# Fills and PSUM copies moved at the norm boundaries of a two-part transformer kernel's second half

## What is computed

```python
def second_block(x, mem, ...):
    mem_n = rms_norm_2(mem, mem_norm_gain)
    for layer in range(DEPTH):
        g = norm_gains[layer]
        hn = rms_norm_2(x, g[0])
        if layer % 2 == 0:
            y = mlstm_mixer(hn, ...)
        else:
            y = stick_breaking_mixer(hn, ...)
        x = x + rms_norm_2(y, g[1])
        y = memory_cross_attention(rms_norm_2(x, g[2]), mem_n, xa_w_q[layer], xa_w_kv[layer], xa_w_o[layer])
        x = x + rms_norm_2(y, g[3])
        y = swiglu_ffn(rms_norm_2(x, g[4]), ffn_w_gate_up[layer], ffn_w_down[layer])
        x = x + rms_norm_2(y, g[5])
    return x

def rms_norm_2(x, gain):
    y = x * lax.rsqrt(jnp.mean(x * x, axis=-1, keepdims=True) + RMS_EPS)
    return y * gain
```

## Time and profile before

| | us |
|---|---|
| median of three runs | 1744.31 |
| their lowest and highest | 1741.27, 1747.47 |
| the profiled execution | 1744.86 |
| its span, first to last instruction | 1743.1 |
| PE busy in the span | 1678.6 |
| DVE, ACT, POOL busy | 1161.3, 949.2, 331.8 |

### The profile page before, as it was taken

One profiled execution on the slowest core, in us unless ns is written; L12 is line 12 of the kernel. 1 busy time (PEld: TensorE's weight loads), 2 busy tenths in 40 slices (PEclk: granted clock), 3 DMA queues, 4 the chain that ended last, 5 costly groups with the idle time before them and its releaser, 6 DMA issues.

```text
span 1743.1 us, 32581 instructions
## 1 busy us (share of the span) xinstructions
PE 1678.6 (96%) x13166; PEld 1605.1 (92%) x13166; DVE 1161.3 (67%) x1964; ACT 949.2 (54%) x1717; POOL 331.8 (19%) x304
## 2 busy tenths in 40 slices
PE   7999999999999989999999999999999998989997
PEld 6998889999997889999999889999989998889996
DVE  7889886555577745556675556666686656476665
ACT  6676765644455646544655545544465644354443
POOL 0100110243412112335111101002232210000025
PEclk9999999999999999999999999999999999989999
DMA  5433334555522245555445434565554352335653
GB/s 203 135 112 122 110 109 146 169 171 177 175 96 79 91 133 195 183 189 185 146 135 167 145 110 157 170 184 188 163 167 143 113 161 97 119 117 168 190 181 108
DMA packets 76325, 257.47 MB, mean 148 GB/s; under 512 B 8464, under 2 KB 12560, under 8 KB 75920
## 3 DMA queue, kind: packets, MB, share of 16 engines
q1 hardware_dynamic: 76176, 255.39, 45.3%
HBM read 254.31 MB, written 1.05 MB: 147 GB/s over the span
## 4 chain that ended last, share of the span: by engine, by line
PE 79%; DVE 11%; ACT 6%; issue 3%; POOL 1%; DMA 0%; POOLq 0%; DVEq 0%; SPq 0%; ACTq 0%
PE pb L140 79%; DVE WL L159 3%; DVE TMP L171 2%; ACT SCR L149 2%; DVE SCR L171 2%; ACT WH L149 1%; ACT L156 1%; PE pb L143 1%; DVE SCR L159 1%; DVE HNL L171 1%; ACT ASH L149 1%; ACT TMP L149 0%; ACT SCR L150 0%; ACT Rbuf L149 0%; DVE ASL L171 0%
## 5 line engine op out<-in xcount | busy, mean ns | idle before, releaser
L159 DVE TENSOR_TENSOR WL<-RAW,WH 128x1024 fp32r<-128x1024 f32 (+4 forms) x514 | 606.6, 1182 | 13.3 <-ACT WH L149 13.0
L140 PE MATMUL pb<-HNH,WH 128*128 128x256 f32 (+1 forms) x2056 | 595.2, 289 | 4.9 <-issue 2.4
L149 ACT ACTIVATE WH<-RAW 128x1024 fp32r<-128x1024 f32 (+4 forms) x514 | 507.5, 989 | 151.1 <-PE pb L140 148.1
L140 PE MATMUL pb<-HNH,WL 128*128 128x256 f32 (+1 forms) x2056 | 584.6, 284 | 0.0
L140 PE MATMUL pb<-HNL,WH 128*128 128x256 f32 (+1 forms) x2056 | 584.4, 284 | 0.0
L140 PE MATMUL pb<-ASH,WH 128*128 128x256 f32 (+1 forms) x1560 | 453.0, 290 | 10.3 <-DVE WL L159 7.7
L140 PE MATMUL pb<-ASH,WL 128*128 128x256 f32 (+1 forms) x1560 | 444.6, 285 | 0.0
L140 PE MATMUL pb<-ASL,WH 128*128 128x256 f32 (+1 forms) x1560 | 444.1, 285 | 0.0
L140 PEld LDWEIGHTS pb<-HNH,WH 128*128 128x128 f32 x2056 | 389.5, 189 | 12.9 <-issue 5.6
L140 PEld LDWEIGHTS pb<-HNH,WL 128*128 128x128 f32 x2056 | 389.9, 190 | 0.0
L140 PEld LDWEIGHTS pb<-HNL,WH 128*128 128x128 f32 x2056 | 388.1, 189 | 1.1
(11 more groups left out here) (155 smaller groups left out, 1735.9 us busy)
## 6 DMA issues: line engine op xcount, KB each, us to landing
RAW<-in_w_gu SPq DMA_DIRECT2D x88, 512.0 KB, 3.9
RAW<-in_w_up SPq DMA_DIRECT2D x64, 512.0 KB, 3.5
RAW<-in_w_down SPq DMA_DIRECT2D x64, 512.0 KB, 3.5
RAW<-in_w_ssd SPq DMA_DIRECT2D x48, 512.0 KB, 3.5
RAW<-in_w_xkv SPq DMA_DIRECT2D x32, 512.0 KB, 3.9
RAW<-in_w_mlin SPq DMA_DIRECT2D x24, 512.0 KB, 3.6
RAW<-in_w_fd SPq DMA_DIRECT2D x32, 384.0 KB, 3.0
RAW<-in_w_sbqkv SPq DMA_DIRECT2D x24, 512.0 KB, 4.1
```

The lines of the kernel that those rows point to most:

```text
L140: return self.eng.matmul(o, l, r, start=start, stop=stop, skip_group_check=skip) if self.eng else Nothing()
L149: return self.eng.activation(o, i, f, bias=bias, scale=scale)
L159: return self.eng.tensor_tensor(o, a, b, op) if self.eng else Nothing()
```

## The change

`FIRSTS` becomes 1, 1, 1, 0 for mlo, xo0, fd0, sbo (before 3, 2, 2, 1), so `pe_rest` stands behind one fill, at sbo behind none. On PE all later fills then come in one run, and behind them all feeds of the next norm. On ACT `act_fill` is taken apart: `act_fill_begin` makes the high splits, `act_fill_end` waits for PE and copies. The splits of the first later fill stand ahead of the norms; behind norms 1, 3, 5, 7 come the copy of a fill and then the splits of the next one. On DVE the low splits of the first later fill stand ahead of the Newton step, those of the others ahead of gains 2, 4, 6. Instructions, data and the order of `PLAN` are the same.

```diff
-        FIRSTS = {"mlo": 3, "xo0": 2, "fd0": 2, "sbo": 1, "xo1": 0, "fd1": 0}
-
-        def fills_at(post, m):
-
-            rest = FILL[post][FIRSTS[post]:]
-            return rest[m // 2:m // 2 + 1] if m % 2 == 0 else []
+        FIRSTS = {"mlo": 1, "xo0": 1, "fd0": 1, "sbo": 0, "xo1": 0, "fd1": 0}
...
-        def act_fill(q, kind, l, m):
+        def act_fill_begin(q, kind, l, m):
             if kind == "k":
-                i, b = act_block(q, f"xkv{l}", 0, m, T2)
+                act_block(q, f"xkv{l}", 0, m, T2)
+            else:
+                act_split(q, v_blocks(q, l, m)[1])
+
+        def act_fill_end(q, kind, l, m):
+            if kind == "k":
+                i = AT[f"xkv{l}", 0, m]
                 q.wait_ge(*use[i])
                 if l:
                     q.wait_ge(*xs_[0, 3])
-                q.activation(KM[:, m, :], b, ACT.Copy).then_inc(*eva(i))
+                q.activation(KM[:, m, :], bank_of(i)[:, 0:T2], ACT.Copy).then_inc(*eva(i))
                 return
...
@@ def pe_post_norm
             pe_rest(q, post, T2)
-            for m in range(8):
-                for f in fills_at(post, m):
-                    pe_fill(q, *f)
-                if m and nxt:
-                    pe_feed(q, nxt, m - 1, T2, rms[post])
-            if nxt:
-                pe_feed(q, nxt, 7, T2, rms[post])
+            for f in fill[FIRSTS[post]:]:
+                pe_fill(q, *f)
+            for m in range(8 if nxt else 0):
+                pe_feed(q, nxt, m, T2, rms[post])
@@ def act_post_norm
-            for m in range(8):
-                for f in fills_at(post, m):
-                    act_fill(q, *f)
-                if m and nxt:
-                    act_norm(q, nxt, m - 1, x_added(post, m - 1), use[AT[HNFREE[nxt]]])
-            if nxt:
-                act_norm(q, nxt, 7, x_added(post, 7), use[AT[HNFREE[nxt]]])
+            for f in fill[:1]:
+                act_fill_begin(q, *f)
+            for m in range(8 if nxt else 0):
+                act_norm(q, nxt, m, x_added(post, m), use[AT[HNFREE[nxt]]])
+                if m % 2:
+                    for f in fill[m // 2:m // 2 + 1]:
+                        act_fill_end(q, *f)
+                    for f in fill[m // 2 + 1:m // 2 + 2]:
+                        act_fill_begin(q, *f)
@@ def dve_post_norm
-            fill, nxt, gi = FILL[post], NEXT[post], GAIN[post]
-            for f in fill[:FIRSTS[post]]:
+            fill, nxt, gi = FILL[post][FIRSTS[post]:], NEXT[post], GAIN[post]
+            for f in FILL[post][:FIRSTS[post]] + fill[:1]:
                 dve_fill(q, *f)
...
-                for f in fills_at(post, m):
-                    dve_fill(q, *f)
+                if m and m % 2 == 0:
+                    for f in fill[m // 2:m // 2 + 1]:
+                        dve_fill(q, *f)
```

More of the change, by code:

```diff
@@ L1821, in act_fill @@
                     q.wait_ge(*xs_[0, 3])
-                q.activation(KM[:, m, :], b, ACT.Copy).then_inc(*eva(i))
+                q.activation(KM[:, m, :], bank_of(i)[:, 0:T2], ACT.Copy).then_inc(*eva(i))
                 return
-            ids = v_blocks(q, l, m)
-            act_split(q, ids[1])
-            q.wait_ge(*use[ids[1]])
+            i = AT[f"xkv{l}", 0, 8 + 2 * m]
+            q.wait_ge(*use[i + 1])
             if l:
@@ L1829, in act_fill @@
             for t in range(2):
-                q.activation(VM[:, t, 256 * m:256 * m + 256], bank_of(ids[t])[:, 0:256], ACT.Copy).then_inc(*eva(ids[t]))
+                q.activation(VM[:, t, 256 * m:256 * m + 256], bank_of(i + t)[:, 0:256], ACT.Copy).then_inc(*eva(i + t))
+        def act_fill(q, *f):
+            act_fill_begin(q, *f)
+            act_fill_end(q, *f)
         def dve_fill(q, kind, l, m):
@@ L1863, in act_post_norm @@
         def act_post_norm(q, post):
-            fill, nxt = FILL[post], NEXT[post]
-            for f in fill[:FIRSTS[post]]:
+            fill, nxt = FILL[post][FIRSTS[post]:], NEXT[post]
+            for f in FILL[post][:FIRSTS[post]]:
                 act_fill(q, *f)
```

## The result

| | before | after |
|---|---|---|
| median of five runs, us | 1745.16 | 1736.58 |
| lowest and highest | 1741.27, 1747.47 | 1735.54, 1738.35 |
| the profiled execution | 1744.86 | 1738.35 |
| its span | 1743.1 | 1736.6 |

The ratio is 0.9954 with a 95% interval of 0.9939 to 0.9969: the changed kernel is faster by 8.6 us, between 5.4 and 10.6. The forecast was 1735.5 in a range of 1730 to 1741.

A forecast was written before the change was run, and what follows sets the result against it. PE, busy 96% of the span, was taken as the bound; gains 4.3 + 2.6 + 3.2 + 0.5 less 1.5 for one clock fall make 9.1 us, from 1744.31 to 1735.2, written as 1735.5, range 1730 to 1741.

The forecast's parts named there:

- xo0, 4.3: At xo0 sums start one block earlier, all five feeds find their squares, gate block ends 1087.1: gain 4.3 us.
- the price of five feeds, 1.66: At xo0 and mlo, five feeds ahead of the gate block counted as 1.66 us of PE work.
- fd0, 2.6: At fd0 the fills' end stays, the fifth feed waits, first block ends 1300.4 instead of 1303.05: gain 2.6 us.
- sbo, 3.2: At sbo sums precede the only fill, Newton starts 1442.65 instead of 1445.84, block ends 3.2 earlier: gain 3.2 us.
- one fall in the whole change: At mlo one fall of the granted clock behind a 2.77 us PE idle, charged at 1.5 us.
- mlo, 0.5 less 1.5 of clock: At mlo earlier sums bring a new 2.77 us PE wait: gain 0.5 us, less 1.5 for a clock fall.
- Rival 1: No clock fall is added at mlo: gain 10.6 us, time 1733.7; chance 0.26.
- rival 2: At xo0, fd0 and sbo DVE slips, and the clock falls a second time: gain 6.1, 1738.2 us; chance 0.20.
- Rival 3: At seven bank hand-overs copies behind the norms hold PE: 14.1 lost against 9.1, 1749.3 us; chance 0.04.
- Rival 4: At fd0 or sbo squares ahead of the first fill are late, Ln not earlier: gain 3.3, 1741.0; chance 0.08.
- three signs of being wrong: PE waits for copies at xo0 or fd0; sbo's first feed over 3 us after the fill; mlo's wait at every fill.

The follow-up runs named there:

- the kernel with filler: The changed kernel with six products of constants, results unused, ahead of mlo's second V fill, where PE waited for the copy; 1735.44 us, ratio 0.9955.

## Why the prediction was right, and where not

The time, 1736.58 against 1735.5, and the sum of 9.1 against 8.6 of the medians, came out within what can be measured. The terms, against the stretches:

- **xo0, 4.3; measured 3.94.** The chain was right: no wait of PE for a bank, a square or HNL, and no fall of the clock. About 1.5 of the gain is the block that ran at half clock before; in the nine kernels with earlier sums the clock did not fall here. The term that was mis-sized is the price of five feeds, 1.66. They take 1.97 (in the full rows 1084.06 to the first gate matmul at 1086.03). I had halved the 0.67 of two products, but two do not cost twice one. A product is two records, and all ten of the five feeds start 0.215 apart; only the last is followed by the gate matmul after 0.03. So n products ahead of a block take 0.215 (2n - 1) + 0.03: 0.67 for two, 1.11 for three (1091.36 to 1092.46 before), 1.97 for five. The same 0.3 is missing at mlo (994.88 to 996.85).
- **fd0, 2.6; measured 2.17.** The fills' end stood still, as said: the first feed is 16.15 after the start of the stretch, 16.05 before. The fifth feed does wait for its square, which ends 1.92 after that point (1.97 in the forecast; its row starts 1294.29 and lasts 0.40), though the grouped row of PE shows no bracket. The block begins at 2.32 (1295.09), as forecast, but takes 3.43 instead of 3.0. That is the 0.4: I had priced a block whose eight chunks all lie ready, and DVE was still writing HNL until 1298.0.
- **sbo, 3.2; measured 2.05, and 3.20 where the clock stayed up** (19.77 - 16.57, the kernel with filler; its sbo is the same code). From the first feed to the tail sums both take 8.07, so the fall in the kernel before cost nothing there. Every link is in the trace: the second split waits 2.02 for ACT, then Newton, then the chain as it was. What failed is the sentence on the clock: I charged one fall in the whole change and wrote of sbo only that it "keeps a stretch of sparse products". Before, the clock fell there too, but under feeds that were waiting anyway; in after it fell under the block. PE alone, of before and then of after:

```profile
1450.00:1452.00 2.00, 2.00 (x6) 0.50 0.00 0
```

```profile
1446.00:1447.00 1.00, 1.00 (x3) 0.62 0.00 0
1447.00:1448.00 1.00, 1.00 (x7) 0.50 0.00 0
1448.00:1449.00 1.00, 1.00 (x7) 0.50 0.00 0
1449.00:1450.00 1.00, 1.00 (x8) 0.67 0.00 0
```

- **mlo, 0.5 less 1.5 of clock, a loss of 1.0; measured 1.30.** The wait was forecast at 2.77 in one piece and is 2.57; the clock's price was 1.5 and is 1.51; the feeds took 0.3 more. That is 1.1, and 0.2 remain from small differences that I did not follow up.

Together 1.1 of sbo's clock, 0.4 at xo0, 0.4 at fd0 and 0.3 at mlo are 2.2, and 9.1 - 2.2 = 6.9 is the sum of the stretches. The medians gave 1.7 more than the stretches do, so that they came within 0.5 of the forecast is in part luck. No experiment settles which part of that is the first half's scatter and which is the clock's at sbo and xo1, where other executions of the same code are up to 1.5 shorter.

**The rivals.** Rival 1 (no fall) and rival 2 (a second fall) were both the right kind: a second fall that costs came, 1.1 at sbo, not at mlo. Rival 3, the ring at every bank, bit once, as the forecast had it; the other hand-over at mlo is 0.52, and xo0 and fd0 have none. Rival 4 is refuted by fd0's 2.17 and by the first feed of sbo 1.0 after the fill. None of the three signs of being wrong came: PE has no wait for a copy at xo0 or fd0, the first feed at sbo is 1.0 behind the fill, and the long wait at mlo does not recur.

**What I did not see** is that one edit of the three carries the gain. I costed the change as a whole at each boundary. Costed by edit, it would have shown the sums ahead of the fills as the gain, the run as 1.5 more, and the late copies as the cause of mlo's loss.

## To carry to other kernels

When a change bundles several moves, price each of them at each place: here one line gave 9.5 us at the boundaries, and the copies that were moved out of the way of the norms gave back 3.6 at the one boundary with two-bank fills behind each other. A copy that frees a bank may be put behind other work only if none of that work waits, by whatever engines, for the user of the bank. A wait of PE costs more than its length when the clock falls behind it, so compare the step of the block behind the wait too.

## What the runs showed of the hardware

- **The clock falls at a different moment in executions of the same instructions.** sbo with after's code took 16.57 (no fall), 17.70, 17.72 and 18.41 us. In the last of these the clock was 0.50 in 1444 to 1448, under the last feed and most of the block:

```profile
1444.00:1448.00 4.00, 3.53 (x15) 0.50 0.00 0
```

xo1, the same code in every kernel, took 14.46 to 14.65 in five and 15.86 to 16.06 in the other five. In after (16.06) the clock was 0.50 from 1530 to 1534, under the last feed and into the block; in the kernel with mlo as before (14.47) it was 0.99 in 1528 to 1530 and 1.00 behind that, under its whole block (from 1528.76). Stretches with no fall repeat to 0.02 us (xo0: 20.45 in six kernels, 20.46 in two more).
- **A float32 product of 256 columns costs 0.43 us at full clock (a matmul of a block: 2.85 / 24 = 0.119), and less as the last ahead of a block.** Its two records start 0.215 apart, in five feeds as in the six products of the experiment (979.18 to 981.55 for twelve starts); a block's first matmul starts 0.03 behind the last record (996.82 to 996.85 in after). Divided by their number, two give 0.33 and five 0.39, which looks like two prices and is one. The six of the experiment can't be priced by the start of the V fill at 981.90: that is set by the copy, and comes as late without them.
